# Ten norms per token, joined streams in the SSD projection, and a reordered opening and FFN ending

## The reference, cut to what matters

```python
def rmsnorm(x, g):                      # 13 of them in the kernel
    return x * lax.rsqrt(jnp.mean(x * x, axis=-1, keepdims=True) + 1e-6) * g
def modulate(x, g, shift, scale): return rmsnorm(x, g) * (1 + scale) + shift
def swiglu(u, wg, wu, wd): return (silu(u @ wg) * (u @ wu)) @ wd     # 1024 -> 2816 -> 1024

# first block: m = silu(c) @ ada_w[i] + ada_b[i]  gives 9 shifts, scales and gates per layer
for i in range(2):
    x = x + 0.5*m[2]*swiglu(modulate(x, ...), ...)
    if i == 0: h = h + 0.5*mc[2]*swiglu(modulate(h, ...), ...)        # h is the context
    u, uc = modulate(x, ...), modulate(h, ...)
    y = ssd_mixer(u, uc)   if i == 0 else pool_mixer(u)   # both streams go through ssd_w_in
    x = x + m[5]*y
    x = x + 0.5*m[8]*swiglu(modulate(x, ...), ...)
x = rmsnorm(x, final_g)
# second block, two layers
for layer in range(2):
    h = rmsnorm(x, pre_norm[layer]); proj = h @ w_in[layer]
    y = concat(gated linear attention, sparse attention) @ w_out[layer]
    x = x + rmsnorm(y, post_norm[layer])
```

## Time and profile before

| | us |
|---|---|
| median of 3 runs | 2337.64 |
| lowest, highest | 2336.06, 2338.97 |
| profiled execution, its own time | 2338.51 |
| span of its trace | 2336.8 |
| TensorE (matmul) busy | 2150.9 (92%) |
| VectorE busy | 1470.1 (63%) |
| ScalarE busy | 989.6 (42%) |
| mean granted TensorE clock | 0.937 |

### The profile page before, as it was taken

One profiled execution on the slowest core, in us unless ns is written; L12 is line 12 of the kernel. 1 busy time (PEld: TensorE's weight loads), 2 busy tenths in 40 slices (PEclk: granted clock), 3 DMA queues, 4 the chain that ended last, 5 costly groups with the idle time before them and its releaser, 6 DMA issues.

```text
span 2336.8 us, 39398 instructions
## 1 busy us (share of the span) xinstructions
PE 2150.9 (92%) x16735; PEld 2051.4 (88%) x16735; DVE 1470.1 (63%) x1814; ACT 989.6 (42%) x1113; POOL 174.5 (7%) x153
## 2 busy tenths in 40 slices
PE   3999999989979899998999899979999899799897
PEld 3899999989949799998999799979998689799867
DVE  2646677779789957776644744457765445676543
ACT  2433455434324644334333533445345334534532
POOL 1000000000010000000000000002300000320000
PEclk7999999999998799999999899989999799899878
DMA  9577768833222347885655255434434033333401
GB/s 332 187 274 269 242 221 292 300 96 110 91 87 96 125 131 261 290 285 200 217 179 179 95 180 181 163 115 151 128 112 145 19 127 127 127 116 122 144 1 55
DMA packets 270790, 383.81 MB, mean 164 GB/s; under 512 B 8441, under 2 KB 230727, under 8 KB 270679
## 3 DMA queue, kind: packets, MB, share of 16 engines
q1 hardware_dynamic: 246983, 293.59, 38.0%
q0 software_dynamic: 22288, 85.02, 10.0%
q10 hardware_dynamic: 1408, 3.59, 0.4%
HBM read 381.06 MB, written 1.11 MB: 164 GB/s over the span
## 4 chain that ended last, share of the span: by engine, by line
PE 78%; DVE 14%; ACT 4%; issue 2%; DMA 2%; POOL 0%; ACTq 0%; DVEq 0%; SPq 0%
PE bank L621 22%; PE bank L622 21%; PE bank L623 21%; DVE w_hl L1676 3%; PE bank L1013 3%; PE bank L634 2%; ACT w_hl L1244 2%; DVE e_long L2009 1%; PE bank L662 1%; DVE e_long L2027 1%; DVE rstd L1686 1%; PE bank L647 1%; DVE conv_acc L1958 1%; DVE scratch L1702 1%; DMA raw<-in_ffn_w_up 1%
## 5 line engine op out<-in xcount | busy, mean ns | idle before, releaser
L1676 DVE TENSOR_TENSOR w_hl<-raw,w_hl 128x2048 fp32r<-128x2048 f32 (+1 forms) x281 | 641.1, 2284 | 454.1 <-ACT w_hl L1244 453.9
L621 PE MATMUL bank<-u_hi,w_hl 128*128 128x256 f32 x2376 | 694.1, 292 | 26.1 <-DVE u_lo L1707 23.9
L622 PE MATMUL bank<-u_lo,w_hl 128*128 128x256 f32 x2376 | 682.0, 287 | 0.0
L623 PE MATMUL bank<-u_hi,w_hl 128*128 128x256 f32 x2376 | 681.6, 287 | 0.0
L1244 ACT ACTIVATE w_hl<-raw 128x2048 fp32r<-128x2048 f32 (+1 forms) x281 | 531.5, 1894 | 225.8 <-PE bank L623 208.5
L621 PEld LDWEIGHTS bank<-u_hi,w_hl 128*128 128x128 f32 x2376 | 464.9, 196 | 42.3 <-issue 35.0
L622 PEld LDWEIGHTS bank<-u_lo,w_hl 128*128 128x128 f32 x2376 | 466.7, 196 | 0.5 <-issue 0.5
L623 PEld LDWEIGHTS bank<-u_hi,w_hl 128*128 128x128 f32 x2376 | 465.8, 196 | 0.0
L621 PE MATMUL bank<-h_hi,w_hl 128*128 128x256 f32 x880 | 251.2, 285 | 13.5 <-DVE h_lo L1765 13.5
L622 PE MATMUL bank<-h_lo,w_hl 128*128 128x256 f32 x880 | 250.1, 284 | 0.0
L623 PE MATMUL bank<-h_hi,w_hl 128*128 128x256 f32 x880 | 249.8, 284 | 0.0
(11 more groups left out here) (339 smaller groups left out, 3473.1 us busy)
## 6 DMA issues: line engine op xcount, KB each, us to landing
ada<-in_ada_w POOLq DMA_DIRECT2D x72, 1024.0 KB, 7.5
raw<-in_w_in SPq DMA_DIRECT2D x60, 1024.0 KB, 5.0
raw<-in_ffn_w_gate SPq DMA_DIRECT2D x55, 1024.0 KB, 7.7
raw<-in_ffn_w_up SPq DMA_DIRECT2D x55, 1024.0 KB, 5.2
raw<-in_ffn_w_down SPq DMA_DIRECT2D x55, 1024.0 KB, 5.2
raw<-in_ssd_w_in SPq DMA_DIRECT2D x20, 1024.0 KB, 5.2
raw<-in_w_out SPq DMA_DIRECT2D x16, 1024.0 KB, 5.1
raw<-in_ssd_w_out SPq DMA_DIRECT2D x8, 1024.0 KB, 5.1
```

What stands on the lines that cost most here:

```text
L621: pe.matmul(out_, wh, xh, start=start, stop=False, skip_group_check=True)
L622: pe.matmul(out_, wh, xl, start=False, stop=False, skip_group_check=True)
L623: return pe.matmul(out_, wl, xh, start=False, stop=stop, skip_group_check=True)
L1676: ve.tensor_tensor(wlo[slot][:, 0:n], raw[slot][:, 0:n], whi[slot][:, 0:n].bitcast(F32), ALU.subtract)\
```

## The change

Four things change together.

1. Ten of the thirteen norms (`BY_TOKEN`; not the two opening ones and not `ctx_ssd`) use `norm_by_token`. The squares become the stationary operand and one column of ones the moving one, so 16 matmuls of one column give the sum per token in 128x2 (two tiles of 128 tokens). Root and reciprocal run on 128x2. Two float32 matmuls, with the reciprocal broadcast as the stationary operand and the identity as the moving one, spread it to 128x256 in the upper half of the same PSUM bank, where `apply` reads it.
2. The opening: GpSimd no longer waits for the inputs before its eight loads; SyncE's first weight chunk waits for the fourth modulation chunk and the second for the seventh; `lo_at(0)` comes ahead of the last modulation copy only, and `lo_at(1)` and `hi_at(1)` after the context stream's apply; a mask's load and its cast come later; GpSimd's ninth and tenth loads wait for weight chunk 1.
3. The last pair of each FFN is written out: gate, up, then the down chunk of the pair before, then the last down chunk, with buffers of their own for the last hidden values (`h_last_hi`, `h_last_lo`) and the order of the two loads changed to match.
4. In the SSD projection the two streams' operands form one 512-column access pattern (`both_hi`, `both_lo`), so each weight block is loaded once and multiplied by both; the banks now hold a block of both streams.

```diff
+BY_TOKEN = {"lat_ssd": 3, "lat_f1": 3, "l1_f0": 3, "l1_pool": 3, "l1_f1": 4, "final": 3, "pre0": 2, "post0": 3,
+            "pre1": 2, "post1": 3}
+NBT = {name: i for i, name in enumerate(BY_TOKEN)}
...
+        streams = nc.alloc_sbuf_tensor_at("streams", [P, 2, (region + 16 * KIB - u_at) // 4], F32R, offset=u_at)
+        both = streams[:, :, 0:2 * KB * T].rearrange("p s (h k t) -> p s h k t", h=2, k=KB)
+        both_hi, both_lo = both[:, :, 0, :, :], both[:, :, 1, :, :]
...
+                if i == 0:
+                    sp.wait_ge(ada_in[3], 16)
                 load(g, cols256(wg, 0), CH)
+                if i == 0:
+                    sp.wait_ge(ada_in[6], 16)
                 load(g + 1, cols256(wu, 0), CH)
...
+                load(g + 3 * FP - 3, cols256(wu, FP - 1), CH)
+                load(g + 3 * FP - 2, wd[:, 2 * FP - 4:2 * FP - 2, :], CH)
                 load(g + 3 * FP - 1, wd[:, 2 * FP - 2:2 * FP, :], CH)
 
             for name, (t, at, n) in ROWS.items():
                 sp.dma_start(rows[at:at + n, t, :], row_src[name]).then_inc(S["rows_in"], 16)
-            sp.wait_ge(ada_in[5], 16)
...
-            pool.wait_ge(S["x_in"], 32)
             for q in range(ADA_FIRST):
                 load_ada(q, q, 0)
...
+            pool.wait_ge(landed[1], 16)
             pool.wait_ge(S["ada_done"], 1)
             for half in range(2):
                 load_ada_half(ADA_FIRST // 2, half, 0)
...
+            def norm_by_token(name):
+
+                n, b = N[name], bank[BY_TOKEN[name]]
+                for k in range(KB):
+                    pe.wait_ge(S["squares"], KB * n + k + 1)
+                    for tile in range(TT):
+                        m = pe.matmul(b[:, tile:tile + 1], scratch[:, k, tile * P:(tile + 1) * P], ones[:, 0:1],
+                                      start=k == 0 and tile == 0, stop=k == KB - 1, skip_group_check=True)
+                m.then_inc(S["stat_done"], 1)
+                pe.wait_ge(S["recip_done"], n + 1)
+                for tile in range(TT):
+                    m = pe.matmul(b[:, T + tile * P:T + (tile + 1) * P],
+                                  rstd[n % 2][:, tile:tile + 1].to_broadcast([P, P]), ident, start=True, stop=True)
+                m.then_inc(S["rstd_spread"], 1)
...
+                def last_pairs(ada_too):
+                    j = FP - 1
+                    pe.wait_ge(S["silu_done"], pairs + j)
+                    hidden(g + 3 * FP - 4, 0)
+                    pe.wait_ge(S["mult_done"], pairs + j)
+                    hidden(g + 3 * FP - 3, 1)
+                    pe.wait_ge(S["h_done"], pairs + j)
+                    down(g + 3 * FP - 2, False, False)
+                    if ada_too == "one":
+                        pe.wait_ge(S["mods_done"], 2 * (m0 - 1) + 2 * j)
+                        ada_turn_one(m0 - 1 + j)
+                    pe.wait_ge(S["h_done"], pairs + FP)
+                    down(g + 3 * FP - 1, False, True, 0, h2_hi, h2_lo)
...
-                m = project(c0 + 1 + i, 4 + 2 * (i % 2), u_hi, u_lo)
-                if i not in (2, 3):
-                    m = project(c0 + 1 + i, 5 + 2 * (i % 2), uc_hi, uc_lo)
+                c = c0 + 1 + i
+                take(c)
+                wh, wl = chunk(c, KB, 256)
+                ns = 1 if i in (2, 3) else 2
+                for blk in range(2):
+                    f = slice(blk * P, (blk + 1) * P)
+                    o = bank[4 + 2 * (i % 2) + blk][:, 0:ns * T].rearrange("p (s t) -> p s t", s=ns)
+                    for k in range(KB):
+                        m = mm3(o, wh[:, k, f], wl[:, k, f], both_hi[:, 0:ns, k, :], both_lo[:, 0:ns, k, :],
+                                k == 0, k == KB - 1)
                 m.then_inc(S["chunk_used"], 1)
...
             hi_at(0)
+            rounded("ctx_f0", uc_hi, shifted(0, 0, 1))
             hi_at(1)
-            rounded("ctx_f0", uc_hi, shifted(0, 0, 1))
+            act.dma_start(mask_in[:, :, :], a["level_masks"].rearrange("p (i t) -> p i t", t=P))\
+                .then_inc(S["mask_in"], 16)
             rounded("lat_f0", u_hi, shifted(0, 0, 0))
...
-                ve.reciprocal(rstd[n % 2][:, :], rms[n % 2][:, :]).then_inc(S["recip_done"], 1)
+                c = slice(0, TT if name in BY_TOKEN else T)
+                ve.reciprocal(rstd[n % 2][:, c], rms[n % 2][:, c]).then_inc(S["recip_done"], 1)
+
+            def spread(name):
+                if name not in BY_TOKEN:
+                    ve.wait_ge(S["recip_done"], N[name] + 1)
+                    return rstd[N[name] % 2][:, :]
+                ve.wait_ge(S["rstd_spread"], NBT[name] + 1)
+                return bank[BY_TOKEN[name]][:, T:2 * T]
...
-                        ve.scalar_tensor_tensor(scratch[:, k, :], src[:, k, :], scale[:, k:k + 1],
-                                                rstd[N[name] % 2][:, :], ALU.mult, ALU.mult).then_inc(S["scaled"], 1)
+                        ve.scalar_tensor_tensor(scratch[:, k, :], r, scale[:, k:k + 1], src[:, k, :],
+                                                ALU.mult, ALU.mult).then_inc(S["scaled"], 1)
...
-                mult(FP)
+                ve.wait_ge(S["h_done"], pairs + FP - 1)
+                mult(FP, g + 3 * FP - 2, h2_hi, h2_lo)
                 lo_at(g + 3 * FP)
+                if ADA_LOOPS[i][-1][2] == "one":
+                    ada_keep_one(m0 - 2 + FP)
                 lo_at(g + 3 * FP + 1)
...
-            lo_at(0)
-            lo_at(1)
             for m in range(ADA_FIRST // 2):
                 if m >= 2:
                     ve.wait_ge(S["ada_turned"], m - 1)
+                if m == ADA_FIRST // 2 - 1:
+                    lo_at(0)
...
             modulation(0, 0, 1)
             apply("ctx_f0", xc, mod_a, shifted(0, 0, 1), uc_hi, uc_lo)
+            lo_at(1)
             modulation(0, 0, 0)
             apply("lat_f0", x, mod_a, shifted(0, 0, 0), u_hi, u_lo)
-            ve.wait_ge(S["mask_in"], 16)
-            ve.tensor_copy(level_mask[:, :, :], mask_in[:, :, :]).then_inc(S["dve_step"], 1)
-            step()
-            ffn(0)
+            ffn(0, masks)
```

More of the change, by code:

```diff
@@ L193, in two_block_kernel @@
         u_at = top[0]
-        u_hi = fixed("u_hi", [P, KB, T], F32R)
-        u_lo = fixed("u_lo", [P, KB, T], F32R)
+        u_hl = fixed("u_hl", [P, 2, KB, T], F32R)
+        u_hi, u_lo = u_hl[:, 0, :, :], u_hl[:, 1, :, :]
         scratch_at = top[0]
@@ L341, in two_block_kernel @@
              "cols_turned", "cols_done", "x_turned", "x_done",
-             "squares", "stat_done", "root_done", "recip_done", "scaled", "u_hi_done", "u_done",
+             "squares", "stat_done", "root_done", "recip_done", "rstd_spread", "scaled", "u_hi_done", "u_done",
              "silu_done", "mult_done", "h_hi_done", "h_done", "y_done",
@@ L370, in two_block_kernel @@
         SSD_COLS = [INNER + 256 * c for c in (8, 9, 10, 11, 0, 1, 2, 3, 4, 5, 6, 7)]
-        CONV_IN = [2, 4, 5, 6] + [6 + 2 * i for i in range(1, 9)]
+        CONV_IN = [2 * i for i in range(1, 13)]
         CONV_SILU = [2, 4, 5, 6] + [6 + i for i in range(1, 9)]
@@ L709, in hidden, with down @@
                     m.then_inc(S["chunk_used"], 1)
-                def down(c, opens, closes, j=0):
+                def down(c, opens, closes, j=0, hh=h_hi, hl=h_lo):
                     take(c, j)
@@ L718, in down @@
                             m = mm3(bank[4 + b // 2][:, (b % 2) * T:(b % 2 + 1) * T], wh[:, kk, f], wl[:, kk, f],
[L719 removed]
+                                    hh[:, kk, :], hl[:, kk, :], opens and kk == 0 and b % 2 == 0,
                                     closes and kk == 1)
@@ L757, in ffn @@
                         pair(1, True, ada_too)
-                    with pe.Fori(max(j0, 2), j1) as j:
+                    with pe.Fori(max(j0, 2), min(j1, FP - 1)) as j:
                         pair(j, False, ada_too)
-                pe.wait_ge(S["h_done"], pairs + FP)
-                down(g + 3 * FP - 1, False, True)
+                last_pairs(ADA_LOOPS[i][-1][2])
             pe.wait_ge(S["consts_in"], 16)
@@ L794, in _ @@
             ffn(1, lambda: norm("ctx_ssd"))
-            norm("lat_ssd")
+            norm_by_token("lat_ssd")
             c0 = G["ssd_in"]
@@ L986, in _ @@
                 m.then_inc(S["pool_done"], 1)
-            norm("l1_f1", 4)
+            norm_by_token("l1_f1")
             ffn(4)
-            norm("final")
+            norm_by_token("final")
             def level(l, i):
@@ L1099, in _ @@
             for l in range(DEPTH):
-                norm(f"pre{l}")
+                norm_by_token(f"pre{l}")
                 g = G[f"proj{l}"]
@@ L1375, in _ @@
                     act.wait_ge(S["conv_done"], i - 1)
-                for s in ((0, 1) if i not in (2, 3) else (0,)):
-                    nc.scalar.activation(cpad[i % 2][:, :, s, PAD:PAD + T],
-                                         bank[4 + s + 2 * (i % 2)][:, :].rearrange("p (b t) -> p b t", b=2),
+                ns = 1 if i in (2, 3) else 2
```

(7 more changed lines are left out.)

86 lines of the change are left out of this document (42 added, 44 removed).

## The result

| | before | after |
|---|---|---|
| median (lowest to highest), us | 2338.30 (2336.06 to 2343.97), 4 runs | 2302.99 (2302.35 to 2305.72), 4 runs |
| profiled execution, its own time | 2338.51 | 2302.35 |
| span of its trace | 2336.8 | 2300.7 |
| mean granted clock | 0.937 | 0.936 |

The ratio is 0.985, 95% interval 0.983 to 0.987. The kernel became 35.3 us faster; 49.9 were forecast. 2303 lies inside the range (2270 to 2306), 15 above the predicted 2288.

What follows compares the result with a forecast made beforehand. TensorE, busy 92% of the span, was taken to bound the kernel, with time in its work and its waits. Savings of 8.5 + 15.7 + 16.5 + 9.2 = 49.9 us gave 2288 for the median, range 2270 to 2306.

Steps and rivals of the forecast that it cites:

- the norm at full clock: Ten norms: last sum to first product takes 1.28 us instead of 2.32; 0.94 net saved for each norm.
- In two of the ten (`pre0`, `pre1`) TensorE will be at 1.2 GHz: Norms: after a long wait the spread's 0.45 us doubles in these two, taking 2 x 0.45 off the gain.
- What was to be given back: Opening: 3.7 us for the delay from `lo_at(1)`, making the third chunk's gap 4.9, and 2.2 of half clock.
- sums start at 29.04 plus whatever the inputs lose ... I take 0.8: Opening: modulation sums start at 29.8, as inputs sharing the DMA engines with GpSimd's loads cost only 0.8 us.
- rival (b): Opening: GpSimd's 8 MB take the engines while inputs still come; TensorE starts 7 us later; 2295; chance 0.10.
- The 4 us that I had worked out for the inputs by an even share: Opening, under rival (b): two queues sharing evenly bring the inputs about 4 us late, of which the tables hide 3.
- these 12.95 MB are there at about 36: Opening: the data needed before the last modulation sum lands at about 36, that sum starts at 38.4; margin 2.4 us.
- what makes 256 columns 0.120 instead of 0.108 (the weights, likely) is hidden: SSD projection: the extra time vanishes at 512 columns, so spacing is 0.216 against 0.240 for two; 9.2 us in all.
- Rival (a): SSD projection: the pairing gives nothing, 512 columns cost 0.240; 2297; chance 0.12.
- the Trainium skill's rule that was weighed in the prediction: SSD projection: spacing N / 2.4 + 2.5 ns at full clock, two of 256 columns 218 ns, one of 512 216.
- the forecast's own, 2278 to 2298: Whole kernel: range in us of the forecast 2288 itself, without its rivals; chance 0.60.
- The bounds: Whole kernel: the parts added at their ends give 2268 and 2310, narrowed to a range of 2270 to 2306.

Runs made afterwards that it cites:

- inputs_first: Changed kernel with GpSimd again waiting for the two inputs before its eight modulation loads; 2303.26 us, against the changed kernel's 2302.99.
- undo_ending: Changed kernel with part 3 undone, the last pair of each FFN in the old order with one pair of buffers; 2319.17 us.
- micro_columns: No part of the model: groups of 48 fp32r matmuls of 128 to 512 columns, other engines streaming or idle; spacings 0.111 to 0.227 us.
- latent_again: The same program as latent_later, run again in a later series; 2293.99 us, ratio to the kernel before 0.9809.
- latent_later: Changed kernel with the latent stream's first modulation, apply and rounding moved behind the first FFN's pair 1; 2294.11 us.
- both_opening: Changed kernel with the edits of latent_later and inputs_first together; 2296.51 us.

## Why the prediction was right, and by which steps less than forecast

**Part 1, 5.5 of 8.5.** The mechanism was right and so was the norm at full clock: 1.30 against 1.28, root and reciprocal 0.17 each against 0.22 and 0.20. `lat_ssd`, `lat_f1`, `l1_f0` and `final` won 0.9 to 1.1. The failed step is "In two of the ten (`pre0`, `pre1`) TensorE will be at 1.2 GHz": in six of the ten the spread took 1.22 or 1.23 instead of 0.72. Of these, `l1_f1`, both `pre` and both `post` norms won only 0.2 to 0.5. In both `pre` norms the sums, too, took 0.25 longer than before (6.96 against 6.71), for which the forecast had 0.1 at most. `l1_pool` even lost 0.3: its sums ran at a granted 0.77 and took 4.6 us against the usual 3.6. From the first sum to the first matmul behind it `l1_pool` took 8.9 us here and 8.5 before. In the nine other kernels with the new norm it took 7.4 or 7.5 six times and 7.8, 7.9 and 8.8 in the rest, so the loss goes with where the clock was low in a trace, and why it was low there is open.

**Part 2, 11.45 of 15.7.** What was to be given back came out within 0.1: gap 4.82, clock 2.25. The failed term is "sums start at 29.04 plus whatever the inputs lose ... I take 0.8": TensorE started 4.6 us late, at 18.3. The first sum was at 33.68 instead of 29.8, which is 3.9 of the 4.3 that the first FFN matmul came late; the other 0.4 are what the pause in the third sum cost (a step of 3.70 instead of 2.85) less what the other steps were shorter. That is rival (b)'s mechanism at two thirds of its price. I took the tables for a fixed floor because nothing but the inputs was shown to compete with them. They are only 0.3 MB in 19 loads (SyncE's list has 19 of them, not the 22 of the description), and with GpSimd's loads beside them the last of them lands later. The second input, too, landed at 15.8 and before at 10.6. The Trainium skill, "DMA: Bandwidth & Descriptors", section "Queues, rings and completion order", says that each engine goes round its queue rows packet by packet. The trace agrees in so far as tables and inputs both came some 5 us later beside the eight loads; it does not show the shares. The 4 us that I had worked out for the inputs by an even share were nearer than my 0.8, and the error was to let the tables hide 3 of them.

The step behind it, "these 12.95 MB are there at about 36", held. The core had moved 12.85 MB by 36 us, the last of the eight chunks had landed at 35.1, and ScalarE began on chunk 0 at once when it came:

```profile
36.17 1.91 ACT L1287 ACTIVATE w_hl<-raw 128x2048 fp32r<-128x2048 f32 x1 [2.01 <-DMA raw<-in_ffn_w_gate]
```

TensorE began the last sum only at 42.74, so the data did not hold it up. (The sum itself is loose: it counts a chunk as 1 MB, where the profile has 8.39 MB for eight. In the profile's unit it is about 13.5 MB, which at 0.35 MB a us are there some 1.5 us later, so the margin was 1 us and not 2.4.) inputs_first is the other case: TensorE is in time and the data is 4 us late, because the loads start 9.8 us later, and the first FFN matmul is at 47.7 again. So each order tried makes either TensorE or its data late. All at once (seven traces: 45.8 to 47.7), all after the inputs (47.7, 47.6) and two ahead of the rest (46.2) come out alike; the seven, all with the same order of loads, differ by as much among themselves. An order that has both early was not found, and bringing the tables in with fewer loads was not tried.

**Part 3, 18.6 of 16.5.** Right, a little more. The five FFNs won 4.3, 2.4, 3.9, 3.8 and 4.2 from their first matmul to the norm behind them (the first one without what part 2 gives back); the gap of 2.4 is in all of them, and four have 1.4 to 1.9 more. In three of these, as counted, it is the half clock of the last down chunk. The fourth is another matter. The stretches of the kernel before, with the last down chunks of the third and fourth FFN:

```profile
1080.60:1087.80 7.20, 7.20 (x48) 7.20 (x49) 6.18 (x8) 5.33 (x7) 0.00 (x0) 0.76 0.37 121
1286.68:1292.50 5.82, 5.82 (x48) 5.76 (x48) 4.72 (x4) 4.32 (x4) 0.00 (x0) 1.00 0.20 58
```

and TensorE's timeline behind the fourth:

```profile
1293.34 0.92 PE L634 MATMUL bank<-scratch,ones 128*128 128x256 f32 x3 [0.69 <-ACT scratch L1257]
```

There the down chunk had its full clock before as well. The 1.4 are the wait for the squares, 0.69 in the record and 0.86 by the starts, which is now gone, and a stretch of 1.2 GHz at that FFN's start that is 1.1 us shorter now, about 0.5 of time. undo_ending brings the waits back and 16.2 us.

**Part 4, 2.3 of 9.2.** The failed step is "what makes 256 columns 0.120 instead of 0.108 (the weights, likely) is hidden" at 512. micro_columns shows 0.0135 in addition to the columns for each matmul, at either width, with new weights or the same. The saving is 0.013 a pair alone and 0.0075 in the kernel (0.2325), and 384 x 0.0075 = 2.9 lies beside the 2.3 found. Rival (a) is what happened, nearly. By the Trainium skill's rule that was weighed in the prediction ("TensorE: Matmul & The Clock Gate", "Back-to-back issue gap") a pair saves one gap of 2.5 ns and the part is worth 1 us. The section gives that rule for a single, isolated matmul, which the prediction left out. Its form, a period a column and a fixed part a matmul, is what micro_columns shows from 256 columns on; its fixed part is five times too small for fp32r (2.5 ns against 13.5). Of the two ways to read the extra 11 ns, as the columns' or as the matmul's, the second is measured, and I had been wrong to let it vanish.

**The rest, -1.8.** In the second block the stretch between the statistics of `osq0` and `post0`, whose code is that of before except for names, took 148.9 us before and 152.8 after. TensorE was busy 1.5 us longer in it and stood still 2.4 longer. Ten us of it, before and after, by stretches:

```profile
1862.80:1872.80 10.00, 9.12 (x50) 6.91 (x49) 5.86 (x9) 2.62 (x5) 0.00 (x0) 1.00 0.01 2
```

```profile
1826.00:1836.00 10.00, 9.12 (x22) 5.01 (x21) 2.77 (x4) 2.29 (x4) 0.00 (x0) 0.62 0.01 2
```

TensorE is busy for 9.12 us in both, but it gets 50 instructions done at a granted 1.00 and 22 at 0.62. How long the clock is low does not decide it: TensorE was at 1.2 GHz for 37.5 us of the stretch before and for 41.0 in the changed kernel, but also for 41.0 in latent_again, which took 149.8, and for 44.4 in inputs_first, which took 150.6. It matters where in the stretch it is low; that this is the whole of the 3.9 us is not shown. Among the kernels run here, all with this same code, the stretch took 148.2 to 149.8 in three of them (undo_ending, latent_later, latent_again), 150.6 and 151.0 in inputs_first and both_opening, and 152.3 to 152.9 in the other five besides the changed one. What sets which, I did not settle: the pairing, the opening and the norms are each undone in a kernel that still has the loss, and undo_ending, which has not, also moves everything behind the first FFN. It is 4 us that a change elsewhere can win or lose, and more than the pairing is worth.

The prediction's range held, and the forecast's own, 2278 to 2298, did not. Parts 1, 2 and 4 fell short by 3.0, 4.3 and 6.9, the rest by 1.8, and only part 3 gave 2.1 more: 13.8 in all, with the result 3 us inside the upper bound. That is partly luck. The bounds were also added up wrongly: the ends that the prediction states (5, 9, 9 and nothing; 13, 19, 19 and 9.6) give 2315 and 2277, and not 2310 and 2268.

## What to carry to other kernels

Before joining matmuls, ask which part of the spacing belongs to the column and which to the instruction: here 256 to 512 columns saves 0.013 us a pair, 5%, and never the 10% that the row of one width seems to offer. A step that waits for small tables is not a floor that other loads leave alone; give what is issued beside them a price. Ask for each order of loads both when the engine is ready and when its data is: here an order that had TensorE ready 5 us earlier had its data 4 us later, and won nothing. Look past the wait that an edit removes for the next one on the same engine: another 9 us came from moving work that the next stage does not read out of the list ahead of what it does.

## What the runs showed of the hardware that was not expected

- fp32r matmuls at full clock: 0.111, 0.120, 0.173 and 0.227 us apart for 128, 256, 384 and 512 columns. The first is above its columns' time by 0.058, the other three by 0.0135. With the same weight block all the time 512 columns stay at 0.227.
- 59.6 us of VectorE and 57.6 us of ScalarE work beside the first seven of the eight kinds of micro_columns change no spacing.
- Two float32 matmuls of 128 columns, four passes in the record: 0.72 us at full clock, 1.22 at a granted 0.50.
- The last of 19 small tables, 0.3 MB in all, landed 4.6 us later when 8 MB were started beside them at once (18.3 against 13.7), and 4.0 later than before with only 2 MB (17.7).
- The same stretch of code took 148.2 to 152.9 us in twelve kernels, at a mean granted clock of 0.85 to 0.87 in it, and the longest times do not go with the lowest clock.
